# PEER layer of a hybrid block: 32 tokens by gathered rows, and up tiles with the table as the stationary side

## What is computed

```python
    expert = jnp.take_along_axis(cand_i, top_pos, axis=-1)      # 8 heads x 16 experts for each token
    gate = jax.nn.softmax(top_s, axis=-1)
    ...
        a = jax.nn.gelu(jnp.einsum('ted,td->te', down[eb], tb).astype(jnp.float32), approximate=False)
        return jnp.einsum('te,ted->td', (a * gb).astype(up.dtype), up[eb])
```

## Time and profile before

| | us |
|---|---|
| median of 3 runs (1044.66 to 1047.95) | 1045.99 |
| profiled execution | 1044.37 |
| its span from first to last instruction | 1042.5 |

### The profile page before, as it was taken

The page is one execution under the profiler, slowest core; times in us unless marked ns, Lnnn a source line. Parts: engine busy times, 40 slices in busy tenths (PEclk is TensorE's granted clock), DMA queues, the critical chain, the costliest instruction groups (busy, mean ns, idle before and its releaser), DMA issues.

```text
span 1042.5 us, 18890 instructions
## 1 busy us (share of the span) xinstructions
PE 1027.5 (99%) x7630; PEld 920.1 (88%) x7630; DVE 788.7 (76%) x1400; ACT 527.1 (51%) x842; POOL 129.9 (12%) x103
## 2 busy tenths in 40 slices
PE   8999999999999999999999999999999999999997
PEld 8987888898799999999999999988888888888885
DVE  5567766846689998868988787698888875555575
ACT  5554545454465564666544444544444445445461
POOL 3000000100068983122000000000000000000000
PEclk9999999999999999999999999999999999999999
DMA  9943335742445667787555555655555556556671
GB/s 319 375 164 101 102 102 162 242 131 86 152 141 190 197 209 259 266 299 261 177 170 181 176 173 179 223 173 171 177 171 177 169 177 189 195 191 192 195 249 41
DMA packets 55095, 195.56 MB, mean 188 GB/s; under 512 B 6881, under 2 KB 7441, under 8 KB 54625
## 3 DMA queue, kind: packets, MB, share of 16 engines
q1 hardware_dynamic: 49536, 178.28, 52.4%
q0 software_dynamic: 4896, 15.55, 4.8%
q10 hardware_dynamic: 576, 0.52, 0.2%
HBM read 192.21 MB, written 1.05 MB: 185 GB/s over the span
## 4 chain that ended last, share of the span: by engine, by line
PE 94%; DMA 3%; DVE 1%; ACT 1%; issue 0%; SPq 0%
PE psG L1536 16%; PE psS L1926 16%; PE psT L1926 16%; PE psG L1538 15%; PE psG L1537 15%; PE psO L1894 1%; DMA raw<-in_down 1%; PE psO L1895 1%; PE psT L1912 1%; PE psS L1538 1%; PE psS L1536 1%; PE psS L1537 1%; PE psO L1818 1%; PE psS L1721 1%; PE psS L1912 1%; PE psO L1744 1%
## 5 line engine op out<-in xcount | busy, mean ns | idle before, releaser
L747 ACT ACTIVATE hi<-raw 128x1024 fp32r<-128x1024 f32 x325 | 343.6, 1059 | 285.9 <-DMA raw<-in_up 182.2
L991 DVE TENSOR_TENSOR lo<-raw,hi 128x1024 fp32r<-128x1024 f32 x291 | 354.4, 1221 | 87.6 <-ACT hi L747 86.6
L1536 PE MATMUL psG<-b_two,hi 128*128 128x240 f32 (+1 forms) x1088 | 303.8, 279 | 1.3 <-ACT H L941 0.8
L1537 PE MATMUL psG<-b_two,hi 128*128 128x240 f32 (+1 forms) x1088 | 299.2, 275 | 0.0
L1538 PE MATMUL psG<-b_two,lo 128*128 128x240 f32 (+1 forms) x1088 | 299.2, 275 | 0.0
L1536 PEld LDWEIGHTS psG<-b_two,hi 128*128 128x128 f32 x1088 | 205.4, 189 | 3.5 <-issue 3.3
L1537 PEld LDWEIGHTS psG<-b_two,hi 128*128 128x128 f32 x1088 | 205.5, 189 | 0.1
L1538 PEld LDWEIGHTS psG<-b_two,lo 128*128 128x128 f32 x1088 | 205.4, 189 | 0.0
L1514 DVE TENSOR_TENSOR act_lo<-H,act_hi 128x256 fp32r<-128x256 f32 x128 | 53.6, 423 | 89.9 <-ACT act_hi L970 89.9
L712 POOL TENSOR_TENSOR lo<-raw,hi 128x1024 fp32r<-128x1024 f32 x34 | 82.8, 2443 | 101.0 <-ACT hi L747 100.4
L941 ACT ACTIVATE H<-psG 128x240 f32<-128x240 f32 x128 | 47.1, 368 | 95.5 <-PE psG L1538 95.0
(11 more groups left out here) (370 smaller groups left out, 1618.9 us busy)
## 6 DMA issues: line engine op xcount, KB each, us to landing
raw<-in_down SPq DMA_DIRECT2D x128, 512.0 KB, 3.6
raw<-in_up SPq DMA_DIRECT2D x128, 512.0 KB, 3.7
raw<-in_w_stream SPq DMA_DIRECT2D x73, 512.0 KB, 4.0
w<-in_w SPq DMA_DIRECT2D x4, 512.0 KB, 12.9
xT<-in_xT SPq DMA_DIRECT2D x4, 256.0 KB, 5.8
memT<-in_memT SPq DMA_DIRECT2D x1, 1024.0 KB, 6.9
x_tok<-in_x_tok POOLq DMA_DIRECT2D x1, 1024.0 KB, 7.9
ln_gb<-in_ln_g POOLq DMA_DIRECT2D x2, 512.0 KB, 7.1
```

The costliest lines, as they stand in the source:

```text
L747: act.activation(hi[hi_slot(n)][:], raw[slot(n)][:], ACT.Copy).then_inc(hi_done, 1)
L991: dve.tensor_tensor(lo[slot(n)][:], raw[slot(n)][:], hi[hi_slot(n)][:].bitcast(FP32), ALU.subtract)\
L1536: pe.matmul(out, hi_l, hi_r, start=start, stop=False)
L1537: pe.matmul(out, hi_l, lo_r, start=False, stop=False)
```

## The change

`APART` becomes 32, in two sets of 16 tokens (`SPAN`, `SETS`), and `SD` 224. Both the down and the up sums of these tokens now come from gathered rows: 32 gathers of down rows (entries 42, 44, .. 72 and 74, 77, .. 119 of the down tiles), and 32 of up rows from up tile 62 on, each weighted and added by DVE into `raised_x` (`raise`, 128x1024). They are summed over heads by matmuls in `last`. `spread`, `apart` and the three-part one-hot go. Gates cover 28 groups, every 17/8 tiles in down and 43/20 in up.

An up tile now has the table chunk as weights: 8 chunks of 128 output columns; in chunks 0 to 5 one matmul of `hi` with 448 moving columns (high and low activations side by side in `act_two`) and one of `lo` with 224, in chunks 6 and 7 three with 224. The sums are transposed (output columns by tokens) and fill 7 banks, so gates in up have one bank of `psO`. After tile 119 the sums are folded: ACT copies the low half, DVE adds the high half into `turned_x`, and PE turns them back with the identity in `last`.

`one2` is made once for a group: POOL saves it to DRAM during the down tiles and loads it back during the up tiles. POOL too now walks `table_order()`.

```diff
-APART_AT = [42 + 2 * k for k in range(APART)]
+APART_AT = [42 + 2 * k for k in range(SPAN)] + [74 + 3 * k for k in range(SPAN)]
+RAISE_AT = [62 + 7 * q // 4 for q in range(APART)]
+GATHER_AHEAD = 5
...
+        if j == FOLDED - 1:
+            out += [("fold", c) for c in range(KD)]
...
+            for what, j in TABLE_ORDER:
+                if what == "gather":
+                    k = j % APART
+                    if j < APART:
+                        pool.wait_ge(tile_used, DOWN + APART_AT[k] - GATHER_AHEAD)
+                    else:
+                        pool.wait_ge(tile_used, UP + RAISE_AT[k] - GATHER_AHEAD)
...
+                elif what == "index":
+                    pool.wait_ge(gate_ready, 1)
+                    for i in range(SETS):
+                        own = slice(P - APART + i * SPAN, P - APART + (i + 1) * SPAN)
+                        for h in range(PH):
+                            pool.dma_start(apart_w[h * SPAN:(h + 1) * SPAN, i, :], chosen_s[own, PH + h, :])\
+                                .then_inc(apart_w_in, 16)
+                    copy_x(1)
+                    save_one2(0)
+                elif what == "gates" and j + 1 < GROUPS:
+                    save_one2(j + 1)
+                elif what == "gates" and j + 1 < 2 * GROUPS:
+                    load_one2(j + 1)
...
+                elif what == "fold" and j < WIDE_CHUNKS:
+                    if j == 0:
+                        act.wait_ge(act_lo, TURNED_H)
+                    act.wait_ge(chunk_done, j + 1)
+                    act.activation(turned_x[:, j, :], chunk_bank(j)[:, SD:2 * SD], ACT.Copy).then_inc(fold_low, 1)
...
+            def fold(c):
+                dve.wait_ge(fold_low, c + 1)
+                dve.tensor_tensor(turned_x[:, c, :], chunk_bank(c)[:, 0:SD], turned_x[:, c, :], ALU.add).then_inc(folded, 1)
...
+                    pe.wait_ge(folded, 2 * (t + 1))
+                    if t == 1:
+                        pe.wait_ge(raised, APART)
+                        for i in range(SETS):
+                            for c in range(2):
+                                pe.matmul(psT[P - APART:P, c * 512:(c + 1) * 512],
+                                          of_token[:, (SETS - 1 - i) * SPAN:(SETS - 1 - i) * SPAN + APART],
+                                          raised_x[i][:, c * 512:(c + 1) * 512], start=i == 0, stop=i == SETS - 1)
...
+                        for k in range(columns[0] * 4, columns[-1] * 4 + 4):
+                            mm = pe.matmul((psS, psT)[t][0:width, k * P:(k + 1) * P], turned_x[:, k, cut], ident[:],
+                                           start=False, stop=k % 4 == 3)
...
-                for t in range(NT):
-                    cut = slice(t * P, (t + 1) * P)
-                    for left, right, st in ((a_hi[j % 4], hi[s], j == 0), (a_hi[j % 4], lo[slot(n)], False),
-                                            (a_lo[j % 4], hi[s], False)):
-                        for c in range(2):
-                            mm = pe.matmul((psS, psT)[t][:, c * 512:(c + 1) * 512], left[:, cut],
-                                           right[:, c * 512:(c + 1) * 512], start=st, stop=False)
+                if j == 0:
+                    pe.wait_ge(h_out, E_TILES)
+                s, two = hi_slot(n), act_two[j % 4]
+                for c in range(KD):
+                    out, cut, st = chunk_bank(c), slice(c * P, (c + 1) * P), j == 0 and c < KD - 1
+                    if c < WIDE_CHUNKS:
+                        pe.matmul(out[:, 0:2 * SD], hi[s][:, cut], two[:].rearrange("p a n -> p (a n)"), start=st, stop=False)
+                        mm = pe.matmul(out[:, 0:SD], lo[slot(n)][:, cut], two[:, 0, :], start=False, stop=j == FOLDED - 1)
+                    else:
+                        mm = three(out[:, 0:SD], hi[s][:, cut], lo[slot(n)][:, cut], two[:, 0, :], two[:, 1, :],
+                                   st, j == FOLDED - 1 and c == KD - 1)
```

More of the change, by code:

```diff
@@ L322, in table_order @@
             out.append(("decode", DECODE_AT.index(j)))
+        if j + GATHER_AHEAD in APART_AT:
+            out.append(("gather", APART_AT.index(j + GATHER_AHEAD)))
         if j in APART_AT:
@@ L326, in table_order @@
             out.append(("dot", APART_AT.index(j - 1)))
[L327 to L330, removed]
+        if j in COEF_AT:
+            out.append(("coef", COEF_AT.index(j)))
         if j == 44:
@@ L716, in _, with load_one2 @@
+            def load_one2(g):
+                s = g % 2
+                if g == GROUPS:
+                    for i in range(2):
+                        pool.wait_ge(one2_out[i], 16 * (GROUPS // 2))
+                pool.wait_ge(gates_done, g - 1)
+                pool.dma_start(one2[s][:].rearrange("p k n b -> p (k n b)"), a["one2"][g - GROUPS]).then_inc(one2_back[s], 16)
             pool.wait_ge(shifted, 1)
[L717 to L718 removed]
+            copy_x(0)
@@ new lines, in raise_rows @@
+            def raise_rows(q):
+                i, k = q // SPAN, q % SPAN
+                dve.wait_ge(rows_in[(APART + q) % ROWS], 16 * ((APART + q) // ROWS + 1))
+                if q == 0:
+                    step.wait()
+                else:
+                    dve.wait_ge(raised, q)
+                if k == 0:
+                    dve.tensor_scalar(raised_x[i][:], rows[(APART + q) % ROWS][:], coefs[:, i, 0:1], None, ALU.mult)\
+                        .then_inc(raised, 1)
+                else:
+                    dve.scalar_tensor_tensor(out=raised_x[i][:], in0=rows[(APART + q) % ROWS][:],
+                                             scalar=coefs[:, i, k:k + 1], in1=raised_x[i][:],
+                                             op0=ALU.mult, op1=ALU.add).then_inc(raised, 1)
@@ L1478, in _ @@
                     product(j)
-                elif what == "spread":
-                    spread_heads()
-                elif what == "apart":
-                    apart_gates()
+                elif what == "coef":
+                    coefficients(j)
+                elif what == "raise":
+                    raise_rows(j)
+                elif what == "fold" and j < WIDE_CHUNKS:
+                    fold(j)
                 elif what == "up":
@@ L1940, in _ @@
                     last(j)
-                elif what == "apart":
-                    pe.wait_ge(spread_ready, 1)
-                    pe.matmul(psS[:, 0:APART], spread[:].rearrange("p h k -> p (h k)"), of_token[:], start=True, stop=True)\
-                        .then_inc(apart_done, 1)
                 elif what == "gates":
```

238 lines of the change are left out of this document (117 added, 121 removed).

## The result

The changed kernel takes 1040.12 us (median of 8 runs, 1037.82 to 1042.38) against 1047.39 for the kernel before on the same chips. The ratio is 0.9932, with a 95% interval of 0.9917 to 0.9947: about 7 us faster. Forecast were 16 us and a time of 1028. So the sign was right, the time lies in the range of 1015 to 1041, and more than half of the gain is missing. The profiled execution took 1037.82 us, span 1036.0, the fastest of the eight.

A forecast was written before the change was run, and what follows sets the result against it. PE, busy 99% of the span, was taken as the bound, so the span is the sum of its matmul steps. The terms summed to -16.3 us against 1044.37, giving 1028.1, forecast as 1028, range 1015 to 1041.

The forecast's parts named there:

- the floor of the steps: Down tiles: loading 128 weight columns sets a floor of 0.112 us a step; 224 columns take 0.1115, -1.5 us.
- the up tiles: Up tiles: 448-column steps of 0.201 and 224-column steps of 0.1115 make 2.54 us for 2.73, -22.8 over 120 tiles.
- the gates: Groups of 16 small gate matmuls on PE: 0.58 us each, 38.1 in all becomes 32.5, -5.6.
- the wait before `last`: After up tile 119: PE waits about 5.3 us for tile 126's load, split and the folds, 0.5 before: +4.8.
- rival by which columns count in full: Down and up matmuls: weight loads hide behind 224 columns, so narrower steps get cheaper; about 1001 us, chance 0.09.
- Down stalls: Down tiles: POOL's small DMAs delay a gather, three gathers then run in a bunch with streamed loads: +3, ends 0 and +10.
- Clock: At `last`: the clock may fall in PE's gap of 5.3 us, costing 0 to 2.3; +1 taken.
- 16 transposes: In `last`: 16 added transposes of 128 f32 columns at 0.108 us each, +1.75.
- Four matmuls of 512 f32 columns: In `last`: four added matmuls at 0.43 us each, +1.7.
- Hand-overs: Rival: DVE near 95% in down, ACT behind `dot`, PE behind the GELU; PE takes DVE's pace, about 1040 us, chance 0.12.
- Queues: Rival: DMA queues bound the raised rows (up tiles 57 to 116, needing 316 GB/s); slower, about 1051 us, chance 0.07.
- The wide matmuls: Rival, up tiles: a 448-column step takes 0.227 us as with 512, 19 us back, about 1047, chance 0.04.

The follow-up runs named there:

- kernel with 128 columns: The kernel before the change, with 128 moving columns in place of 240 in 18 of the 24 matmuls of each down tile: ratio 0.9997.
- the kernel with the folds put back: Changed kernel with x_apart copies singly, ln_last early, raised rows seven tiles earlier, one2 made by DVE twice; folds of chunks 0 and 1 behind act_two 123: 1035.06 us.

## Why the prediction was half right

The sign, the floor of the steps, the up tiles and the gates came out. The step that failed is the price of the f32 matmuls at the end: the forecast counted the 16 transposes and the four matmuls of the apart tokens at 3.5 us, and they took 7.1. The next is the wait before `last`, which left out DVE's backlog (+4.8 forecast, +6.7 measured).

**Floor of the down steps: right.** Rows of the changed kernel's down tiles, 224 columns:

```profile
561.42 0.11 PE psG L1589
561.53 0.12 PE psG L1590
...
563.09 0.11 PE psG L1589
```

15 steps take 1.67 us, 0.111 each (0.112 as the mean of all down tiles); a tile takes 2.68 us against 2.69. The rival by which columns count in full is dead for 224, and for 128. The rule of the Trainium skill that was set beside it ("TensorE: Matmul & The Clock Gate", section "Back-to-back issue gap") had 96 ns for 224 columns; the trace disagrees. The Trainium skill's section "LDWEIGHTS (loading the stationary operand)" on the same page was nearer: it has 107 ns, and the trace shows 112 at the full clock. At half the clock the step is 213 (kernel with 128 columns). That the load of the weights makes the floor is inferred: 240, 224 and 128 columns take the same step, but no run changed the weights; the rows with 64 weight columns point the same way.

**Up tiles: right.** 2.55 us for 2.54, with steps of 0.21 and 0.10 in turn:

```profile
963.96 0.21 PE psS L1990
964.17 0.10 PE psS L1991
964.27 0.21 PE psT L1990
964.48 0.10 PE psT L1991
```

The hundredth of a us makes 1.2 us over 120 tiles, of which 0.5 is the forecast's own rounding: unrounded its tile is 2.544, which saves 22.3 and not 22.8. Stalls were 2.9 us for 1.6 forecast (the first tile's 0.70 for 0.6, and waits for `lo` of 0.69, 0.38 and 1.09 for 1). A group of gates costs 0.58 in up, as forecast: tiles of 3.05 and 2.63 in turn where two without gates take 5.10.

**Down stalls: right in size, by luck as far as the runs tell.** 4.5 us against 1.7 before, +2.8 for a forecast of +3. The given reason, bunched gathers behind POOL's small DMAs, was at best part of it: spreading the small ones moved the stall, and it moved with the eight `x_apart` copies, which the forecast had priced at their issue (0.48 each) and not at what they do to the queues. But one at a time they took no stalls away when this was the only edit, so the cause is not shown. Some 1.2 us of the down stage's difference I can't place; it is within that stage's scatter.

**The end: 6.4 us short, in four terms.**

- *Wait before `last`, +4.8 forecast, +6.7 measured* (7.1 against 0.4 before). The kind of wait stands: without raised rows it is 5.4, with them moved earlier 5.6, for a forecast of 5.3, though by the load of tile 125 and not of 126. What the step left out is DVE's backlog, 1.8 us. The forecast took the load's 4.37 us from the kernel before, where no gathers ran beside it; in the changed one tile 118 took 8.15 us to land, DVE stood idle for 2.8 us and then had one raised row of 1.2 us among its splits. Whether two busy resources keep up had been asked for the raised stretch (2.32 of 2.54 us on DVE, 316 GB/s) but not for the 20 us behind it, where six raw tiles are asked for within some 5 us.
- *Clock, +1 forecast, +1.3 measured.* Right, but the 1 was picked between 0 and 2.3, and after waits of 5.5 and 5.4 us the first pass grew by 1.5 and 2.1 (the kernel with the folds put back, the one without raised rows).
- *16 transposes, +1.75 forecast, 3.54 measured* (1.78, 0.87 and 0.89). *Four matmuls of 512 f32 columns, +1.7 forecast, 3.55 measured.* This is the mis-sized term, 3.6 us, the largest single part of what is missing, and the step of the forecast that failed. The price came from the earlier trace rows, 1.73 us for "x8". I read eight matmuls; the source has four at that line, and each plain f32 matmul stands as two instructions in the trace. So 128 columns cost 0.22, not 0.11, and 512 cost 0.89, not 0.43. The run with BF16 sums, where four are four and take 0.97 us, bears this out for the four; the transposes weren't tested by a run of their own, and their 3.54 is read from the chain.

Added up: 1.9 + 0.3 + 1.8 + 1.85 = 5.9 of 6.4 in the end. Another 0.4 is the 48 matmuls of the second tokens, 5.72 + 5.60 us where the kernel before had 10.93, which the forecast had taken as unchanged. With 2.3 in up and 1.0 in down the stretches miss by 9.7, and -16.3 + 9.7 = -6.6 for a measured -6.5 in the spans. The median's gain, 7.3, is within their spread.

**The rivals.** Hand-overs: neither DVE nor ACT set PE's pace in the stages; at the end DVE did. The time of about 1040 that this rival gave was met by another road, which is luck. Queues: at a share of 0.90 to 0.94 and 320 to 336 GB/s (940 to 970 us) the raised stretch held; the tiles kept 2.55 us but for the three waits, which went with the raised rows. The wide matmuls paid. The forecast named "if PE waits for H around down tiles 50 to 56" as a sign against it, and it came true for 3.4 us.

**`one2` in DRAM** was costed at nothing. It cost 2 to 3 us where it could be measured best. DVE had the time to make it (an estimated 2.74 of 2.81 us a tile, and PE waited for it no more than before); that the saves and loads cost their time in the queues is likely but wasn't traced to a wait.

## What to carry to other kernels

Before taking a price from a group of records, count the instructions in the source: here a plain f32 matmul is two of them, and its price per matmul is twice the mean. When the work on the critical engine shrinks at the end of a stage, add up what the other engines and the queues have still to do from there on: moving one step in the order only pays down to that sum. Where PE has to wait, matmuls that keep it busy can pay for themselves by the clock (1.3 us here). Transfers are to be priced by what waits for the queues too, and not by their issue alone.

## What the hardware showed that I had not expected

- A matmul step with its own 128x128 f32 weights takes 0.112 us at the full clock whether 240, 224 or 128 columns move, and 0.213 at half the clock.
- A plain f32 matmul of 512 columns costs 0.89 us and stands as two instructions; a BF16 one of 512 columns costs 0.24 (0.97 for four).
- Dense matmuls didn't bring the clock back at once: in the kernel with 128 columns it fell after a stall of 1.4 us and was at half for 58 us. The changed kernel, with 224, had a stall of 1.8 us in the same place and kept 1.00. The narrow matmuls saved nothing in the step, and the profiled run took 28 us more than the fastest of its kernel; the kernel before, in the same series, never ran above 1052.1. Which of its properties makes the difference wasn't tried.
- In the 5 us in which eight copies of 64 KB onto 16 partitions, a gather and the streamed tiles met, the queues were at a share of 1.03 with 243 GB/s; streams of whole tiles reached 419 GB/s at that share. Which of the transfers makes the difference wasn't tried alone.
- A 512 KB gather every 4.5 us and a 512 KB tile every 2.55 us held 320 to 336 GB/s over 30 us.
